# Blocked inverse of a delta-rule scan: six doubling levels on 64-row blocks, with the previous step's state products placed inside them

## The reference

```python
def step(S, inp):
    w_t, k_t, v_t, kk_t, b_t = inp[:5]
    sa = jnp.einsum('bhvk,bhk->bhv', S, kk_t)
    S = (S * w_t[:, :, None, :] - sa[..., None] * b_t[:, :, None, :]
         + v_t[..., None] * k_t[:, :, None, :])
    o = jnp.einsum('bhvk,bhk->bhv', S, inp[5]) if with_out else None
    return S, o
S, o = lax.scan(step, S0, xs, reverse=reverse)
```

## Time and profile before

| | |
|---|---|
| median of 3 runs | 4887.59 us (4884.92 to 4891.51) |
| profiled execution, its own time | 4889.43 us |
| its span in the trace | 4887.6 us |
| mean granted TensorE clock | 0.979 |
| TensorE busy | 4685.7 us, 96% of the span |
| DVE, ACT, POOL busy | 2548.3, 1869.2, 428.3 us |
| level products (L1258 with b_G, b_X, b_Y, b_Mr) | 3 x 1920 instructions, 305.9, 305.5 and 300.7 us |
| level joins on DVE (L1475) | 480, 689 ns each |
| level copies on ACT (L1138, L1134) | 480 and 400, 597 and 600 ns each |

### The profile page before, as it was taken

How to read it: one execution, slowest core, us unless ns; L and a number is a source line. 1 busy time by engine, 2 the same in 40 slices (tenths; PEclk the granted TensorE clock), 3 DMA queues, 4 the chain that set the end, 5 groups by cost and what they waited for, 6 DMA issues and landing times. The chain is left out here.

```text
span 4887.6 us, 68771 instructions
## 1 busy us (share of the span) xinstructions
PE 4685.7 (96%) x28888; PEld 3835.9 (78%) x28888; DVE 2548.3 (52%) x3698; ACT 1869.2 (38%) x3156; POOL 428.3 (9%) x347
## 2 busy tenths in 40 slices
PE   8999999999999999999999889899999679999999
PEld 5888877779889998989998644488777457888887
DVE  3245554546435555555555477555443755555543
ACT  3234443445235554555455433311233653111111
POOL 0000000000022322232322100000010000000000
PEclk9999999999989999999999999999999989999999
DMA  5334334334321011011100253343120021221232
GB/s 202 114 137 146 137 139 149 136 140 157 137 84 48 14 52 56 14 61 47 40 35 1 72 167 110 117 138 126 65 79 30 14 108 44 76 72 72 82 108 91
DMA packets 149074, 441.92 MB, mean 90 GB/s; under 512 B 16400, under 2 KB 46352, under 8 KB 131488
## 3 DMA queue, kind: packets, MB, share of 16 engines
q1 hardware_dynamic: 133712, 383.98, 22.2%
q0 software_dynamic: 9296, 32.58, 1.9%
q10 hardware_dynamic: 5760, 20.97, 1.2%
HBM read 294.86 MB, written 141.56 MB: 89 GB/s over the span
## 5 line engine op out<-in xcount | busy, mean ns | idle before, releaser
L172 PE MATMUL pr_ps<-uhl,w_split 128*128 128x512 f32 (+1 forms) x1520 | 585.8, 385 | 3.1 <-DVE w_split L144 2.2
L176 PE MATMUL pr_ps<-uhl,w_split 128*128 128x512 f32 (+1 forms) x1520 | 570.8, 376 | 0.0
L175 PE MATMUL pr_ps<-uhl,w_split 128*128 128x512 f32 (+1 forms) x1520 | 570.4, 375 | 0.0
L1475 DVE TENSOR_TENSOR b_G<-b_ps,cst 128x512 fp32r<-128x512 f32 x480 | 327.6, 689 | 326.3 <-PE b_ps L1258 325.7
L137 ACT ACTIVATE w_split<-share 128x2048 fp32r<-128x2048 f32 x64 | 122.6, 1915 | 703.2 <-DVE ou_vc L3173 271.5
L172 PEld LDWEIGHTS pr_ps<-uhl,w_split 128*128 128x128 f32 x1520 | 286.5, 189 | 81.7 <-issue 29.2
L1134 ACT ACTIVATE b_X<-b_ps 128x512 fp32r<-128x512 f32 x400 | 240.2, 600 | 240.9 <-PE b_ps L1258 240.9
L175 PEld LDWEIGHTS pr_ps<-uhl,w_split 128*128 128x128 f32 x1520 | 286.7, 189 | 55.8 <-issue 5.8
L176 PEld LDWEIGHTS pr_ps<-uhl,w_split 128*128 128x128 f32 x1520 | 286.5, 188 | 52.5
L1138 ACT ACTIVATE b_Y<-b_ps 128x512 fp32r<-128x512 f32 x480 | 286.5, 597 | 88.6 <-PE b_ps L1258 88.6
L1258 PE MATMUL b_ps<-b_G,b_Y 128*128 128x128 f32 x1920 | 305.9, 286 | 13.5 <-DVE b_G L1475 13.2
(11 more groups left out here) (475 smaller groups left out, 10114.1 us busy)
## 6 DMA issues: line engine op xcount, KB each, us to landing
w_ring<-in_w_in SPq DMA_DIRECT2D x41, 1024.0 KB, 5.1
proj<-pr_stage SPq DMA_DIRECT2D x160, 256.0 KB, 2.0
share<-in_w_up SPq DMA_DIRECT2D x24, 1024.0 KB, 4.7
ar<-share SPq DMA_DIRECT2D x32, 512.0 KB, 2.8
b_AR<-ar SPq DMA_DIRECT2D x16, 1024.0 KB, 12.0
pr_raw<-proj SPq DMA_DIRECT2D x48, 256.5 KB, 3.5
ada<-in_ada_w SPq DMA_DIRECT2D x24, 512.0 KB, 5.5
ff<-ou_vc ACTq DMA_DIRECT2D x24, 512.0 KB, 2.6
```

The lines of the kernel that those rows point to most:

```text
L172: mm = nc.tensor.matmul(dst, a[0], b[0], start=start, stop=False)
L175: nc.tensor.matmul(dst, a[0], b[1], start=False, stop=False)
L176: return nc.tensor.matmul(dst, a[1], b[0], start=False, stop=stop)
L1475: L[x]["dve"].done(V.tensor_tensor(Gs[x][:], heads(x, 0), rep(K(f"lev{m}"), 4), ALU.mult), f"{n}.G{m}")
```

## The change

Levels 1 to 5 never mix the two halves of 64 rows, so their matrices are block-diagonal. The change computes only the two diagonal 64x64 blocks b = 0, 1 of each. X, Y0, the join's result (new tile `Gb`) and Y (new tile `Yb`) are now [128, 4, 64], block b on partitions 64b to 64b+63. A quad becomes eight products of 64 rows, 64 columns and 64 moving columns, b alternating, so the row halves of the array alternate; both write PSUM partitions 0 to 63, in different banks. Each copy and join becomes two, one for each block. Level 6 joins the two halves: one corner block of each matrix, four products for G and four for Y, the join a multiplication by -1, one copy into the corner of the full Y. The other corner stays the zero that set-up writes.

G and X of a direction now share two banks (256 columns each in banks 0 and 1), and Y of both directions lie in bank 2 of both, so that `y_next` of one direction waits for the copy of the other's. MakV moves to bank 2, Z to columns 256 to 511 of bank 3.

`states` is gone. The previous unit's steps run inside this unit's levels: `local` behind g(1) of levels 1 to 4 and `carried` behind x(1), state for odd m and output for even m, k = (m-1)//2. DVE's `state` moves before the joins of levels 2 and 4, its `out` behind those of level 5; ACT's `out` behind the copies of level 5. `mean` moves from level 1 of unit 0 to level 2 of unit 1, `variance` to level 5 of unit 1. The last unit's steps run behind the loop.

```diff
-        X = [sb(f"X{x}", [P, 4, P], F32R) for x in range(2)]
-        Y0 = [sb(f"Y0{x}", [P, 4, P], F32R) for x in range(2)]
+        X = [sb(f"X{x}", [P, 4, 64], F32R) for x in range(2)]
+        Y0 = [sb(f"Y0{x}", [P, 4, 64], F32R) for x in range(2)]
+        Yb = [sb(f"Yb{x}", [P, 4, 64], F32R) for x in range(2)]
         Y = [sb(f"Y{x}", [P, 4, P], F32R) for x in range(2)]
+        Gb = [sb(f"Gb{x}", [P, 4, 64], F32R) for x in range(2)]
...
+        rows = lambda b: slice(64 * b, 64 * b + 64)
+        low = lambda x, b, f: ps[0:64, 4 * x + b, f:f + 256].rearrange("p (q f) -> p q f", q=4)
+        g_at = lambda x, b: low(x, b, 0)
+        x_at = lambda x, b: low(x, b, 256)
+        y_at = lambda x, b: low((x + b) % 2, 2, 256 * b)
+        src, dst = [0, 1], [1, 0]
...
-                        F[x]["pool"].done(tt(Y0[x][:], tri[x][e][:], rep(K("lev0"), 4), ALU.mult), f"{n}.Y0")
+                        for b, name in enumerate(("Y0a", "Y0")):
+                            F[x]["pool"].done(tt(Y0[x][rows(b)], tri[x][e][rows(b), :, rows(b)], rep(K("lev0")[rows(b), 0:64], 4), ALU.mult), f"{n}.{name}")
+                            F[x]["pool"].wait(pool, i, f"{n}.{name}")
...
                 def x_out(i, n, x, m):
                     L[x]["pe"].wait(act, i, f"{n}.X{m}")
-                    L[x]["act"].done(A(X[x][:], heads(x, 1), ACT.Copy), f"{n}.X{m}")
+                    for b, name in enumerate((f"X{m}a", f"X{m}")):
+                        L[x]["act"].done(A(X[x][rows(b)], x_at(x, b), ACT.Copy), f"{n}.{name}")
...
                     for q in range(4):
-                        mm = mmul(bank(x, 1)[:, q * P:(q + 1) * P], Y0[x][:, q], ident_r[:], start=True, stop=True)
+                        for b in range(2):
+                            mm = mmul(x_at(x, b)[:, q], Y0[x][rows(b), q], ident_r[rows(b), rows(b)], start=True, stop=True)
                     F[x]["pe"].done(mm, f"{n}.XT")
...
+                def blocks(at_, lhsT, rhs):
+                    for q in range(4):
+                        for b in range(2):
+                            mm = mmul(at_(b)[:, q], lhsT(b)[:, q], rhs(b)[:, q], start=True, stop=True)
+                    return mm
...
-                    L[x]["pe"].done(quad(bank(x, 0), Mr[x], X[x]), f"{n}.G{m}")
+                    if m < last:
+                        mm = blocks(lambda b: g_at(x, b), lambda b: Mr[x][rows(b), :, rows(b)], lambda b: X[x][rows(b)])
+                    else:
+                        mm = corner(g_at(x, 0), Mr[x][rows(src[x]), :, rows(dst[x])], X[x][rows(src[x])])
+                    L[x]["pe"].done(mm, f"{n}.G{m}")
...
+                    if x == 1 and m < last:
+                        L[0]["act"].wait(pe, i, f"{n}.Y{m}")
+                    if x == 0 and m > 1:
+                        L[1]["act"].wait(pe, i, f"{n}.Y{m - 1}")
...
                 def levels(i, n):
+                    i_, n_ = before(i, n)
                     for m in lev:
                         g(i, n, 0, m)
                         if m > 1:
                             y_next(i, n, 1, m - 1)
                         g(i, n, 1, m)
+                        if i_ >= 0 and m < 5:
+                            local(i_, n_, m)
+                        if i and n == 1 and m == 2:
+                            mean(i - 1)
+                        if i and n == 1 and m == 5:
+                            variance(i - 1)
                         if m < last:
                             x_next(i, n, 0, m)
                             y_next(i, n, 0, m)
                             x_next(i, n, 1, m)
...
+                        if i_ >= 0 and m < 5:
+                            carried(i_, n_, m)
...
                 def join(i, n, x, m):
                     L[x]["pe"].wait(dve, i, f"{n}.G{m}")
-                    L[x]["dve"].done(V.tensor_tensor(Gs[x][:], heads(x, 0), rep(K(f"lev{m}"), 4), ALU.mult), f"{n}.G{m}")
+                    if m == last:
+                        L[x]["dve"].done(V.tensor_scalar(Gb[x][rows(dst[x])], g_at(x, 0), -1.0, None, ALU.mult), f"{n}.G{m}")
+                    else:
+                        for b, name in enumerate((f"G{m}a", f"G{m}")):
+                            L[x]["dve"].done(V.tensor_tensor(Gb[x][rows(b)], g_at(x, b), rep(K(f"lev{m}")[0:64, 0:64], 4), ALU.mult), f"{n}.{name}")
...
                 for i, n in UNITS_B:
...
                     passing(i, n, 0)
                     passing(i, n, 1)
-                    for k in range(2):
-                        states(i, n, k)
+                for m in range(1, 5):
+                    local(HP - 1, 4, m)
+                    carried(HP - 1, 4, m)
```

More of the change, by code:

```diff
@@ L894 @@
     ["ident", "ident64", "heads64", "after", "from", "before", "upto", "chunk", "rot", "ahead", "behind", "up", "down",
-     "row", "rest"] + [f"lev{m}" for m in range(7)])}
+     "row", "rest"] + [f"lev{m}" for m in range(6)])}
 def constants():
@@ L1154, in _ @@
                 for i, n in UNITS_B:
-                    nxt = after(i, n)
+                    nxt, (i_, n_) = after(i, n), before(i, n)
                     for m in range(1, last):
@@ L1159, in _ @@
                             y_out(i, n, x, m)
+                    if n_ in (1, 2):
+                        for x in range(2):
+                            out(i_, n_, x)
                     for x in range(2):
@@ L1172, in _ @@
                             start_out(*nxt, x)
-                    if n in (1, 2):
-                        for x in range(2):
-                            out(i, n, x)
                 dve_t.wait(act, HP - 1, "omu")
@@ L1196, in variance @@
                     pool_t.wait(pe, i, "osq")
+                    if i + 1 < HP:
+                        for x in range(2):
+                            B[x]["dve"].wait(pe, i + 1, "0.S1")
                     over_heads(i, osq, "var")
@@ L1258, in quad, with corner @@
                         mm = mmul(bk[:, q * P:(q + 1) * P], lhsT[:, q], rhs[:, q], start=True, stop=True)
+                    return mm
[3 more added lines that the diff above has]
+                            mm = mmul(at_(b)[:, q], lhsT(b)[:, q], rhs(b)[:, q], start=True, stop=True)
+                    return mm
+                def corner(out_, lhsT, rhs):
+                    for q in range(4):
+                        mm = mmul(out_[:, q], lhsT[:, q], rhs[:, q], start=True, stop=True)
                     return mm
@@ L1272, in x_next @@
                         L[x]["act"].wait(pe, i, f"{n}.Y{m - 1}")
-                    L[x]["pe"].done(quad(bank(x, 1), Y0[x] if m == 1 else Y[x], Gs[x]), f"{n}.X{m}")
+                    was = Y0[x] if m == 1 else Yb[x]
+                    L[x]["pe"].done(blocks(lambda b: x_at(x, b), lambda b: was[rows(b)], lambda b: Gb[x][rows(b)]), f"{n}.X{m}")
                 def y_next(i, n, x, m):
                     i_, n_ = before(i, n)
-                    if m == 1 and i_ >= 0:
-                        B[x]["dve"].wait(pe, i_, f"{n_}.S1" if n_ < 4 else f"{n_}.S0")
                     if m == last:
@@ L1293, in levels @@
                             x_next(i, n, 1, m)
-                        if m == 1 and i and n == 0:
-                            mean(i - 1)
-                        if m == 1 and i and n == 1:
-                            for x in range(2):
-                                B[x]["dve"].wait(pe, i, "0.QT")
-                            variance(i - 1)
+                        if i_ >= 0 and m < 5:
+                            carried(i_, n_, m)
                 def solve(i, n, x):
@@ L1369, in out_carried @@
                     s = (2 * n + k) % 2
-                    if not passes(n, k):
-                        B[x]["dve"].wait(pe, i, f"{n}.S0")
                     for h in range(2):
@@ L1511, in _ @@
                         step(0, 0, x)
+                for x in range(2):
+                    zero(0, x)
                 for i, n in UNITS_B:
-                    nxt = after(i, n)
-                    if n == 0:
-                        for x in range(2):
-                            zero(i, x)
+                    nxt, (i_, n_) = after(i, n), before(i, n)
                     for m in lev:
+                        if i_ >= 0 and (m == 2 or m == 4 and n_ < 4):
+                            for x in range(2):
+                                state(i_, n_, x, m // 2 - 1)
                         for x in range(2):
                             join(i, n, x, m)
+                        if m == 5 and n_ > 2 and i_ >= 0:
+                            for x in range(2):
+                                out(i_, n_, x)
+                            if n == 0:
+                                for x in range(2):
+                                    zero(i, x)
                         if i and (n, m) in tail:
@@ L1533, in _ @@
                         passed(i, n, x)
-                    for k in range(1 if n == 4 else 2):
-                        for x in range(2):
-                            state(i, n, x, k)
```

(7 more changed lines are left out.)

84 lines of the change are left out of this document (52 added, 32 removed).

## The result

Over four runs the changed kernel takes **5233.3 us** (5231.6 to 5236.5), the kernel before 4886.3: ratio 1.071, with an interval of 1.069 to 1.073. It is slower, as forecast, but by 347 us where 73 were forecast, and outside the range. Its profiled execution has a span of 5232.6 us and a mean granted clock of 0.875 (0.979 before). Of the kernels further down, one (fill256) had three runs more than 1.5% slower than its fourth, at a lower granted clock; its ratio goes by the fourth alone.

What follows compares the result with a forecast made beforehand. TensorE was busy 96% of the span; after the change a level would be bound by its chain of products and copies. From 4889.4 us, -128 at the full clock and +196 for lost clock gave 4957, forecast 4960, range 4755 to 5100.

Steps and rivals of the forecast that it cites:

- the carried products: Carried state and output parts (0.23 and 0.44 us) behind X and Y cost nothing, as long as ScalarE's copy covers them.
- A block quad: Eight 64-row products on TensorE take 0.23 us of issue, in place of 0.46, and 0.44 from first start to last end.
- rival 3: fp32r products in the two row halves don't overlap, each quad stays at 0.46 us: 4890 to 4930 us; chance 0.05.
- A change of shape: Each change of array shape on TensorE costs 0.15 us; eight, less quad savings, add 0.3 us to a unit's middle.
- The evictions: Half copies out of PSUM cost what 128x256 ones cost: 0.53 us a pair on ScalarE, a DVE join ends after 0.74.
- Local products on the path in full: Local products between G of direction 1 and X lengthen the level fully: 0.76 us a state, 1.17 an output.
- Levels 17.1 us at full clock: A unit's levels after an output step, with the moved products inside, sum to 17.1 us, against 15.61 before.
- The first unit, 8 us more: The scan's first unit, already at half clock, gains 8 us more, as quarter-size quads no longer fill TensorE.
- The clock falls in most units: Clock falls in the last two levels, returns within the Gram products: 4.9 us a unit, 196 for 40.
- rival 2: Clock falls in the first levels and stays down through all: 5.3 us a unit more, 5170 us; chance 0.2.
- The sum: Whole kernel: 4889.4 - 128 (full clock) + 196 (lost clock) = 4957 us, forecast as 4960.
- The states alone as a gain: Moving state and output products off the path between units saves 20.0 us a pair.

Runs made afterwards that it cites:

- fill256: fill512 with 256 moving columns in each filler product in place of 512: 5084.7 us in one run, 5163.8 to 5165.7 in the three others.
- fill512: Changed kernel plus unread filler, two fp32 products of 512 moving columns behind the carried products of levels 1 to 5: 4955.6 us.
- states_only: Kernel before, 128-row quads kept, only the state and output products moved into the next unit's levels: 4910.7 us, ratio 1.003 to 1.006.
- fill_mix: fill512 with 256 filler columns in most levels, 768 in level 5 and in levels without moved products, 256 in level 6: 5047.1 us.

## Why the prediction was wrong, point by point

The step that failed is the place of the clock's fall: the prediction has it in the last two levels, so that a unit pays 4.9 us, and the runs show it in the second level, so that 20.32 of 24.96 us of levels run at 0.50. Two terms were mis-sized beside it: the half copies (0.80 us a pair for 0.53), and the carried products, put at nothing.

- **A block quad, 0.23 us of issue and 0.44 to its end:** right (0.25 and 0.42), so rival 3 (the row halves don't overlap) is out.
- **A change of shape, 0.15 us:** about right; a quad with the carried products behind it takes 0.35 us (2604.32 to 2604.67), 0.10 more than one with another quad behind it. The +0.3 us for the middle was wrong: 13.46 at full clock against 13.47.
- **The evictions, 0.53 us a pair on ScalarE and 0.74 for a join:** mis-sized. They take 0.80 and 0.87. What failed is "which cost what 128x256 costs": it took the pitch from rows where all copies have the same rows. So ScalarE has 3.2 us of copies in a level, not 2.1.
- **Local products on the path in full:** wrong in its size. About half of a local output lay beside the join, and at another place they cost 1.8 us a unit more. The carried ones were put at nothing "as long as that copy covers them". In the levels at the half clock it doesn't: an output costs 1.04 us (2610.00 to 2611.04). At the full clock it could not be seen, as TensorE was the bound wherever the clock held.
- **Levels 17.1 us at full clock:** not reached in any run with the blocks. Its first level took 3.19 us for 2.77. fill512 has 20.89 with about 4.5 us of filler, so without it they would lie between 16.4 and 20.9 (an estimate from that level's rows); which, no run can tell, as the clock doesn't hold without the filler.
- **The first unit, 8 us more:** right; its levels went from 27.5 to 19.4 us, at 0.50 in both kernels.
- **The clock falls in most units:** the right mechanism, and the step that decided the size. "The last two levels ... so there it should fall", with the return within the Gram products, was wrong at both ends. It fell in the second level, 4.64 us into the unit, stayed down for 20.32 of 24.96 us of levels, and reached 0.71 on average in the middle. That is rival 2, for which I gave 5170 us and a chance of 0.2; the range, up to 5100, took in only half of it. I had the fp32 products moved into four of six levels hold the clock there. They didn't: 20.3 us with such products, at 19.86 us busy, stayed at 0.50.
- **The sum:** 4957 + 5.3 x 40 is the 5170 of rival 2. The 63 us left over are 1.6 us a unit, and they lie in the levels. By rival 2 a unit's levels would be 17.1 + 0.4 + 5.3 = 22.8 us, and they are 24.96; its middle would be 13.47 + 0.3 + 3.3 + 1.2 = 18.27, and it is 18.21. Over a pair the levels are 12 us over that sum, the middles 4 under it. The carried products alone are more than the 2.2 us of these levels: two outputs at 1.04 us and a state at 0.62 (2614.93 to 2615.55). That they are the reason is argued from the rows; no run takes them out alone.
- **The states alone as a gain:** wrong. states_only is 23 us slower, since full quads leave TensorE no idle time in the levels.

The Trainium skill (TensorE: Matmul & The Clock Gate, "Why this matters for your kernels") has the clock return once the engine is kept busy without long gaps. Here TensorE was busy for 19.86 of 20.32 us at 0.50, as it was for 34.10 of 34.10 before; busy time alone does not bring it back.

## What to carry to other kernels

A change that makes TensorE's work smaller or its waits longer has to be costed at both clocks: look first at whether the clock row of the stretch stands near an edge (here one stretch at 0.50 with the very same quads), and if it does, test it with work that nobody reads before building the change. Price a split copy by rows of the trace in which the rows change too: two copies of 64 rows by 256 elements that alternate between the halves took 0.80 us, where the one copy of 128 by 512 that they replace took 0.48. And work moved into a stretch where an engine is already full, at the clock that it will have then, is not hidden.

## What the runs showed of the hardware that was not expected

- Adding products that nobody reads made the kernel 278 us faster (5233.3 to 4955.6), with the mean granted clock up from 0.875 to 0.974.
- Cutting each X copy of the levels in two on ScalarE, with TensorE's work untouched, cost 461 us (4887.5 to 5348.5), most of it by the clock, 0.57 in most levels.
- A copy overlaps the one ahead only if it starts on the same rows: 0.26 to 0.29 against 0.38 to 0.39 us on ScalarE, 0.33 to 0.35 against 0.42 to 0.44 on VectorE, for 256 elements. From 128 rows to rows 0-63 the first row is the same, and so is the overlap.
- Small changes of the filler move the fall of the clock to other units or from the levels to the middle (fill_mix against fill256), so a variant's time hangs on where in a unit the clock is lost as much as on its work.
